# Twelve slots for the expert weights instead of eight, and a turn's buffers packed into 3592 columns

## What is computed

```python
xl = xl + g1l * (jnp.concatenate([a_lat, b_lat, c_lat], axis=-1) @ w_out[layer])
h2l = (rms_norm(xl, norm2_gain[layer]) * (1.0 + sc2l) + sh2l).reshape(-1, D_MODEL)
...
def hierarchical_moe(h, w_rg, b_rg, w_re, b_re, w_gate, w_up, w_down):
    g_logits = h @ w_rg + b_rg
    ...
    for gi in range(N_GROUPS):
        hid = jax.nn.silu(jnp.einsum('nd,edf->nef', h, w_gate[gi])) * jnp.einsum('nd,edf->nef', h, w_up[gi])
        y = y + jnp.einsum('nef,efd->nd', hid * comb[:, gi, :, None], w_down[gi])
    return y
```

## Time and profile before

| | |
|---|---|
| Median of 3 runs | 2015.53 us (2015.18 to 2016.91) |
| The profiled execution | 2014.9 us, its span 2013.1 us |
| Busy, share of the span | PE 85%, PEld 66%, DVE 43%, ACT 30%, POOL 6% |
| Moved by DMA | 419.94 MB, of it 417.87 MB on SP's queue |
| Mean granted TensorE clock | 0.936 |

### The profile page before, as it was taken

The page is one execution under the profiler, slowest core; times in us unless marked ns, Lnnn a source line. Parts: engine busy times, 40 slices in busy tenths (PEclk is TensorE's granted clock), DMA queues, the critical chain, the costliest instruction groups (busy, mean ns, idle before and its releaser), DMA issues.

```text
span 2013.1 us, 32404 instructions
## 1 busy us (share of the span) xinstructions
PE 1717.4 (85%) x14363; PEld 1325.0 (66%) x14363; DVE 868.9 (43%) x1199; ACT 596.6 (30%) x761; POOL 114.8 (6%) x103
## 2 busy tenths in 40 slices
PE   6999899999899989999999998696987666666665
PEld 6999898998699988899757554486854222122221
DVE  3445556663443556566414735867623111011111
ACT  4345445443334434554321020333313010000100
POOL 0500000000140000000032400000000000000000
PEclk9999999999899999999989998798998888888888
DMA  8651366745675236686333110000085999999998
GB/s 283 220 180 64 126 225 230 273 182 176 227 257 175 79 127 231 243 299 226 128 52 126 42 47 6 2 3 2 4 309 198 409 409 410 410 409 410 410 410 328
DMA packets 154814, 419.94 MB, mean 209 GB/s; under 512 B 13906, under 2 KB 20749, under 8 KB 151618
## 3 DMA queue, kind: packets, MB, share of 16 engines
q1 hardware_dynamic: 154402, 417.87, 56.1%
q10 hardware_dynamic: 288, 0.22, 0.0%
HBM read 416.18 MB, written 1.89 MB: 208 GB/s over the span
## 4 chain that ended last, share of the span: by engine, by line
PE 58%; DMA 17%; DVE 10%; SPq 7%; ACT 5%; issue 3%; DVEq 0%; ACTq 0%
PE bank L1174 28%; DMA wring<-w_exp_up 8%; SPq L1083 7%; DMA R<-w_exp_down 4%; PE ps_s L1284 3%; PE ps_t L1284 3%; PE bank L1362 3%; PE bank L1337 3%; PE ps_s L1337 3%; ACT w_high L1774 2%; DVE w_low L2178 2%; PE ps_t L1344 1%; DMA wring<-w_in 1%; PE bank L1729 1%; DMA wring<-w_up 1%
## 5 line engine op out<-in xcount | busy, mean ns | idle before, releaser
L2178 DVE TENSOR_TENSOR w_low<-wring,w_high 128x2048 fp32r<-128x2048 f32 (+1 forms) x128 | 287.2, 2244 | 330.9 <-ACT w_high L1774 330.2
L1774 ACT ACTIVATE w_high<-wring 128x2048 fp32r<-128x2048 f32 (+1 forms) x128 | 238.1, 1860 | 359.0 <-PE bank L1174 304.5
L1174 PE MATMUL bank<-x_high,w_high 128*128 128x256 f32 x1600 | 325.6, 285 | 18.3 <-DVEq L2206 11.5
L1174 PE MATMUL bank<-x_low,w_high 128*128 128x256 f32 x1600 | 321.6, 283 | 0.0
L1174 PE MATMUL bank<-x_high,w_low 128*128 128x256 f32 x1600 | 319.6, 281 | 0.0
L1174 PEld LDWEIGHTS bank<-x_high,w_high 128*128 128x128 f32 x1600 | 247.2, 191 | 25.9 <-DVEq L2206 12.5
L1174 PEld LDWEIGHTS bank<-x_high,w_low 128*128 128x128 f32 x1600 | 247.7, 190 | 0.0
L1174 PEld LDWEIGHTS bank<-x_low,w_high 128*128 128x128 f32 x1600 | 246.7, 190 | 0.0
L1729 PE MATMUL bank<-R 128*32 128x512 f32 x512 | 69.5, 674 | 38.8 <-DMA R<-w_exp_up 27.7
L1729 PE MATMUL bank<-wring,R 128*32 128x512 f32 x512 | 70.3, 685 | 34.6 <-DMA wring<-w_exp_up 34.6
L2827 DVE TENSOR_TENSOR R<-bank,R 128x512 f32<-128x512 f32 x8 | 5.5, 692 | 202.6 <-PE bank L1729 202.6
(11 more groups left out here) (581 smaller groups left out, 2759.6 us busy)
## 6 DMA issues: line engine op xcount, KB each, us to landing
wring<-w_in SPq DMA_DIRECT2D x37, 2048.0 KB, 8.0
wring<-w_up SPq DMA_DIRECT2D x22, 2048.0 KB, 8.2
R<-w_exp_gate SPq DMA_DIRECT2D x16, 2048.0 KB, 23.4
wring<-w_exp_gate SPq DMA_DIRECT2D x16, 2048.0 KB, 23.9
R<-w_exp_up SPq DMA_DIRECT2D x16, 2048.0 KB, 23.6
wring<-w_exp_up SPq DMA_DIRECT2D x16, 2048.0 KB, 24.1
R<-w_exp_down SPq DMA_DIRECT2D x16, 2048.0 KB, 23.6
wring<-w_exp_down SPq DMA_DIRECT2D x16, 2048.0 KB, 24.0
```

The costliest lines, as they stand in the source:

```text
L1174: mm = pe.matmul(b[:, i * S:(i + 1) * S], left, right, start=k == 0 and m == 0 and i == 0, stop=k == last and m == 2, skip_group_check=True)
L1774: a.activation(high_of(l, job), half_block(l, job, wring), ACT.Copy).then_inc(w_high_ready, 1)
L2178: v.tensor_tensor(half_block(l, job, w_low), half_block(l, job, wring), high_of(l, job).bitcast(F32), ALU.subtract).then_inc(w_low_ready, 1)
```

## The change

It raises `SLOTS_X` from 8 to 12. Slots 4 to 11 are now the last eight pieces of 4096 columns of R, which leaves 3592 columns for all that a turn needs. So the layout is rearranged:

- What a turn needs lies first in R: `gmoe` (the second half of the old `gmul`), `mod2`, `mulT`, then from `turn_area` on `xg`, `comb`, `posm`, `slot_no`, `pcol`, `ccol`, `pick`, `put`, `putT`, `hid`. `yg` shares its columns with `xg`; `sg` and `hidT` share theirs with `hid`. They overlay constants of the mixers (`base`) and `mixtok`.
- The router's buffers (`rl`, the selection, `moe_c`) start at `route_area` and lie in slot 11, `h2T` behind them in slots 11 and 10.
- The constants `c2_moe` come in two copies on ACT's queue, since `slot_no` now lies apart.
- DVE's markers are 3, 1, 2 as before, then 1 once `yb_ready` is reached, 2 and 1 in the output projection, 1 after the router's logits, and 1 after the first dispatch, behind a wait for `xs3_ready`: 12 in all. The first dispatch waits for the memset ahead of it, which now writes `pick`.
- `EXPERT_ORDER` names the slots in the order in which they come free.

```diff
-SLOTS, SLOTS_X = 4, 8
+SLOTS, SLOTS_X = 4, 12
...
-EXPERT_ORDER = (4, 2, 3, 5, 6, 7, 0, 1)
+EXPERT_ORDER = (4, 2, 3, 5, 6, 7, 8, 0, 9, 1, 10, 11)
...
         at[0] = 0
+        gmoe = part(D)
+        mod2 = part(2, KT)
+        mulT = part(3, KT)
+        turn_area = at[0]
         base = part(P + 64 + 18 * 64)
...
-        gmul = part(2, D)
+        gmix = part(D)
...
-        at[0] = x_area
-        h2T = part(KT, S)
+        at[0] = route_area
         rl = part(ST, 36)
...
+        ring_more = [R[:, R_SIZE - (i + 1) * BLOCK:R_SIZE - i * BLOCK] for i in range(more)]
+        assert at[0] <= R_SIZE - (more - 1) * BLOCK, (at[0], "router")
+        h2T = part(KT, S)
+        assert at[0] <= x_area
+
+
+        at[0] = turn_area
+        xg = part(KT, P)
+        yg = xg[:, :, :].rearrange("p k s -> p (k s)")
+        comb, posm = part(ST, N_EXP + QUAD), part(ST, N_EXP + QUAD)
...
-        xg = part(KT, P)
-        sg, hid = part(D_EXP), part(D_EXP)
-        hidT = part(D_EXP // P, P)
-        yg = part(D)
...
+        hid = part(D_EXP)
+        sg, hidT = hid, hid.rearrange("p (k s) -> p k s", k=D_EXP // P)
         assert at[0] <= R_SIZE - more * BLOCK, (at[0], "experts")
...
-            pe.wait_ge(moe_c_in, 16)
+            pe.wait_ge(moe_c_in, 32)
...
-            a.dma_start(moe_c, d["c2_moe"]).then_inc(moe_c_in, 16)
+            a.dma_start(moe_c, d["c2_moe"][:, 0:2 * P + S // SLOTS_E]).then_inc(moe_c_in, 16)
+            a.dma_start(slot_no, d["c2_moe"][:, 2 * P + S // SLOTS_E:]).then_inc(moe_c_in, 16)
...
             v.tensor_tensor(yv, yv, gg[:, :, :], ALU.mult).then_inc(yb_ready, 1)
+            v.wait_ge(yb_ready, 1)
+            v.memset(st[:, 61:62], 0.0).then_inc(moe_used, 1)
...
                 if j % 2 == 1:
-                    v.memset(st[:, 61:62], 0.0).then_inc(moe_used, 1)
+                    v.memset(st[:, 61:62], 0.0).then_inc(moe_used, 2 if j == 1 else 1)
...
             wait_emptied2(v, ("rt", 0))
+            v.memset(st[:, 61:62], 0.0).then_inc(moe_used, 1)
...
-            v.memset(st[:, 60:61], 0.0).then_inc(y_done, 4)
+            v.memset(pick[:, 0, 0:1], 0.0).then_inc(y_done, 4)
+            v.wait_ge(y_done, 4)
             dispatch(slice(0, QUAD))
+            v.wait_ge(xs3_ready, 2)
+            v.memset(order[:, 0:1], 0.0).then_inc(moe_used, 1)
```

More of the change, by code:

```diff
@@ L419, in second_constants @@
     moe[:, P:2 * P] = 1.0
-    moe[:, 2 * P:2 * P + SLOTS_E] = np.arange(SLOTS_E)
-    moe[:, 2 * P + SLOTS_E:] = SLOTS_E * np.arange(S // SLOTS_E)
+    moe[:, 2 * P:2 * P + S // SLOTS_E] = SLOTS_E * np.arange(S // SLOTS_E)
+    moe[:, 2 * P + S // SLOTS_E:] = np.arange(SLOTS_E)
     return {"c2_base": base, "c2_attn": attn, "c2_levels": hg, "c2_moe": moe}
@@ L647, in build @@
         rw_mask = base[:, P + 64:P + 64 + 18 * 64].rearrange("p (m t) -> p m t", t=64)
+        mixtok = part(ST, 768)
         cols2 = part(N_VEC2)
-        gmul = part(2, D)
+        gmix = part(D)
         lng = part(2, 64)
@@ L653, in build @@
         rbias = part(40)
-        mod2 = part(2, KT)
-        mulT = part(3, KT)
         gain2 = part(KT)
@@ L661, in build @@
         gup = part(B_W)
-        mixtok = part(ST, 768)
         st = part(80)
@@ L666, in build @@
         kam = part(2)
+        route_area = at[0]
         pB_r, pB_k, pB_v = part(2, S), part(2, T2), part(2, T2)
@@ L764, in build @@
         assert at[0] <= r_area
-        at[0] = x_area
-        h2T = part(KT, S)
+        at[0] = route_area
         rl = part(ST, 36)
-        comb = part(ST, N_EXP + QUAD)
         gsel, ge, gmx = part(ST, MG), part(ST, MG), part(ST)
@@ L772, in build @@
         sel1, sel2, m2, order = part(ST, PER_GROUP), part(ST, PER_GROUP), part(ST), part(PER_GROUP)
-        sel, posm = part(ST, N_EXP), part(ST, N_EXP + QUAD)
+        sel = part(ST, N_EXP)
         over = part(S // SLOTS_E)
         most, sweeps_f = part(1), part(1)
+        moe_c = part(2 * P + S // SLOTS_E)
+        earlier, all_ones, sweep_from = moe_c[:, 0:P], moe_c[:, P:2 * P], moe_c[:, 2 * P:]
+        more = SLOTS_X - SLOTS
+        ring_more = [R[:, R_SIZE - (i + 1) * BLOCK:R_SIZE - i * BLOCK] for i in range(more)]
[6 more added lines that the diff above has]
+        comb, posm = part(ST, N_EXP + QUAD), part(ST, N_EXP + QUAD)
         sweeps_i = part(1).bitcast(mybir.dt.int32)
-        moe_c = part(2 * P + SLOTS_E + S // SLOTS_E)
-        earlier, all_ones, slot_no = moe_c[:, 0:P], moe_c[:, P:2 * P], moe_c[:, 2 * P:2 * P + SLOTS_E]
-        sweep_from = moe_c[:, 2 * P + SLOTS_E:]
+        slot_no = part(SLOTS_E)
         pcol, ccol = part(ST, QUAD), part(ST, QUAD)
@@ L782, in build @@
         putT = part(ST, P)
-        xg = part(KT, P)
-        sg, hid = part(D_EXP), part(D_EXP)
-        hidT = part(D_EXP // P, P)
-        yg = part(D)
-        more = SLOTS_X - SLOTS
-        ring_more = [R[:, R_SIZE - (i + 1) * BLOCK:R_SIZE - i * BLOCK] for i in range(more)]
+        hid = part(D_EXP)
+        sg, hidT = hid, hid.rearrange("p (k s) -> p k s", k=D_EXP // P)
         assert at[0] <= R_SIZE - more * BLOCK, (at[0], "experts")
@@ L1903, in _ @@
                         for t in range(ST):
-                            a.activation(gmul[:, t, :], ctxb[:, t, :], ACT.Square, accum_out=st[:, 4 + t:5 + t]).then_inc(sumsq2, 1)
+                            a.activation((gmix, gmoe)[t], ctxb[:, t, :], ACT.Square, accum_out=st[:, 4 + t:5 + t]).then_inc(sumsq2, 1)
                     if l == DEPTH - 1 and j == 18:
@@ L2720, in _ @@
                 c = slice(half * 512, half * 512 + 512)
-                chain(v.tensor_tensor(tm, full_bank(("wout", j)), gmul[:, 0, c], ALU.mult))
+                chain(v.tensor_tensor(tm, full_bank(("wout", j)), gmix[:, c], ALU.mult))
                 v.tensor_tensor(h[:, t, c], h[:, t, c], tm, ALU.add).then_inc(dve_emptied2, 1)
```

4 lines of the change are left out of this document (2 added, 2 removed).

## The result

The changed kernel takes **1996.55 us** (median of 4 runs, 1991.78 to 1999.37) where the kernel before took 2015.55 on the same chip (4 runs, 2015.18 to 2016.91): a ratio of 0.990 with a 95% interval of 0.9887 to 0.9914, or 19.0 us less. The profiled execution took 1991.78 us, with a span of 1990.0, 23.1 us less than the span before. The forecast was 1995.2 us in a range of 1993.0 to 2000.5, so the median is within it (the profiled run alone, at 1991.78, is not).

The account below looks back on a forecast made before the run. The expert stage was taken as bound by its DMA bytes, 5.12 us per block. Four blocks (-20.5) and new steps (+0.2) took the profiled 2014.9 to 1994.6 us; 0.6 for the median gave 1995.2, range 1993.0 to 2000.5.

Parts of the forecast that it names:

- Four blocks, 20.5 us: Expert stage's load stream: 84 instead of 88 blocks remain from 1548 us on, 4 x 5.12 = 20.5 us less.
- load 12: One of the expert stage's 96 block loads, numbered 0 to 95; first to wait for an expert matmul, issued 1548.0 us.
- All four are moved in idle time: Before the first expert matmul: loads 6 to 11 fit between slot releases and 1548 us, with 4.4 us to spare.
- a last gap: Load queue just before the steady stream: empty for about 4.4 us before the load issued at 1548.0 us.
- The slack of load 11: Load into the last slot, issued at 1537.8 us: could go as late as 1543.6 without loss, 5.8 us of slack.
- The new steps, +0.2 us: DVE's added waits and markers: those behind router logits and at the first dispatch together cost 0.2 us, the others nothing.
- The constants, nothing: Two copies on ACT's queue instead of one: landed by about 1523.4 us, needed at 1532.84, so no cost.
- The sum, -20.3 us: Whole kernel: -20.5 us for the blocks and +0.2 us for DVE's new steps.
- B: Rival at SP's in-order loads: the last slot comes too late; losing a whole block gives 2000.3 us; chance 0.07.
- C: Rival at the expert loop's entry: code fetches wait behind the full DMA, 2018.9 us; chance 0.07.
- D: Rival at the slot markers: one is miscounted and nothing is loaded early, 2015.7 us; chance 0.01.
- the tail and the spread of runs: Term of the forecast's lower bound, for the kernel's end and scatter between runs: 1.0 us.

Follow-up runs that it names:

- dose runs: Changed kernel with 8, 10 or 12 blocks loaded before PE's first release: 467.5, 457.2 and 446.9 us from first expert matmul to the end.
- e8_hold11: Changed kernel with load 11 held until PE has done the first turn's gather and transposes: 1999.22 us, one run.
- e1_twelve: The changed kernel again without any edit, beside the other versions on their chip: 1995.63 us, ratio 0.990 to the kernel before.
- e10_twelve_b: The changed kernel again without any edit, in a later set on another chip: 1996.19 us, ratio 0.991 to the kernel before.
- e7_hold10: Changed kernel with loads 10 and 11 held until PE has used block 0: 2005.37 us, one run.
- e6_delay6: Changed kernel plus six DVE multiplications that nothing reads, ahead of the first dispatch: 1999.67 us, ratio 0.992 to the kernel before.
- e4_warm: Changed kernel plus unread PE matmuls, 15 before the token places and 6 before the first gather: 2000.37 us, ratio 0.992 to the kernel before.
- e9_warm7_b: Changed kernel plus 7 and 3 unread PE matmuls before token places and first gather, second set: 1994.71 us, ratio 0.990 to the kernel before.
- e5_warm7: Changed kernel plus 7 and 3 unread PE matmuls before token places and first gather, first set: 1994.11 us, ratio 0.989 to the kernel before.
- e3_packed8: Changed kernel's new layout with eight slots and the old slot order and markers: 2015.75 us, ratio 1.000 to the kernel before.

## Why the prediction was right

**Four blocks, 20.5 us: right.** From load 12's issue to the last landing the changed kernel takes 434.03 us where load 8 before took 454.32: 20.29 less for 84 blocks instead of 88. The dose runs put the block at 5.15 us.

**All four are moved in idle time: right**, as every issue that bears on it fell within 0.2 us of its place. I had a last gap of about 4.4 us and the windows show 4.7. The slack of load 11 was given as 5.8 us and is near 5.3, and here the prediction had a slip: 1552.2 - 8.6 = 1543.6 is the time at which load 12, not load 11, would have to be issued to follow without a gap. Load 11 delays load 12's landing (1556.6) only if it lands after 1556.6 - 5.12 = 1551.5, so if it is issued after 1542.9. From 1537.8 that is 5.1 us of slack, close to what e8_hold11 shows. No loss came of it, since load 11 went at 1534.8.

**The new steps, +0.2 us: right.** Load 12 is 2.80 us earlier than before where the loads ahead of it are 2.97 earlier: 0.17 us lost. From the start of L2803 to that of L2820, over the memset and the dispatch, DVE needs 1534.22 - 1532.85 = 1.37 us, against 1.27 before. The marker of the readout (1507.22) stands ahead of 4.32 us of waiting and costs nothing, as said; that behind the logits (1523.03) costs no more than 0.01.

**The constants, nothing: right, though they landed much later.** Both copies were beside the bulk loads on the way:

```profile
L2083 ACTq DMA_DIRECT2D R<-c_moe x1: 345/345/345, 1508.9 to 1508.9; - x1
...
DMA to landing us min/median/max: 6.3/6.3/6.3
L2084 ACTq DMA_DIRECT2D R<-c_moe x1: 450/450/450, 1509.3 to 1509.3; - x1
...
DMA to landing us min/median/max: 7.3/7.3/7.3
```

They landed after 6.3 and 7.3 us, with load 5 and load 6 on the way. The 3.4 us of before were not those of a quiet queue either, but the end of load 5 was all that was left there (it landed at 1514.9); 1509.3 + 7.3 = 1516.6, against a need at 1529.85. I had allowed for the whole of load 6 in front of them, 1523.4 on the axis of before.

**The sum, -20.3 us.** Between the two traces the part from load 3 to the end is 20.1 us shorter. The other 3.0 us of the 23.1 are not the change's: they arise before load 3, and the same changed kernel issues load 0 at 1466.6 in e1_twelve and at 1464.0 in e10_twelve_b, where it is 1461.0 in this trace and 1464.3 in that of before. The time at half clock before 1455 us doesn't explain them: it is 99.0 us in this trace and 105.8 in that of before, but e8_hold11, with only 95.6, issues load 0 at 1465.1, and e7_hold10, with 109.2, at 1464.7. Their cause stays open. The medians of three sets differ by 19.0, 20.0 and 18.0 us, and lie 0.4 to 1.4 us above the forecast's 1995.2. The Trainium skill's fit ("DMA: Bandwidth & Descriptors", "Anatomy of one DMA — SWDGE (gpsimd) path") would have made a block worth 6.8 us, and the whole 27.2. It is a fit for one DMA of the gpsimd path. These runs show that it can't be added up over SP's queued loads: they land 5.12 us apart in the trace and cost 5.15 us each in the dose runs.

**The rivals.** B (last slot late) didn't occur, but e8_hold11 shows its mechanism: load 11 issued 7.0 us later moved the last packet by 1.7. C (engines late into the loop) is false: PE's idle time ahead of the gather is 3.04 against 2.94 us, the first expert matmul 2.96 us earlier rather than later, and the turn after it starts after 2.50 us (2.49 before). So no stall at the loop's entry shows here, even with the DMA full. "Runtime: NRT & Kernel Launch" in the Trainium skill, "Instruction fetch mechanics", describes one for a taken branch whose target isn't in the fetched window; whether it lay outside here no row tells. D is false by the SP timeline.

**What was off is the spread.** I took 2015.18 to 2016.91 for the scatter of a run. In larger sets the kernel before runs from 2011.4 to 2021.1, and the changed one from 1991.8 to 1999.9. The range still held the median, but the profiled run fell 1.2 us below its lower bound, and 1.0 us for "the tail and the spread of runs" was too small. The upper bound of 2000.5 isn't the sum of its terms either: 1995.2 + 1.4 + 0.3 and a whole block of 5.1 give 2002.0. The highest run of the changed kernel was 1999.9. I had looked at the clock only as a mean.

## What to carry to other kernels

When a stage is bound by its bytes, as this one is, more buffers are worth just the blocks that they let in while the queue would otherwise stand, and nothing once it runs full; find the gap in the DMA share, find what ends it, and count the blocks that fit into it with their landing. After such a change the bottleneck ahead of the stage is another one: here the router's path, which had 18 us of empty queue behind it and now costs one us for each us that is added to it (taking 3.65 us off gave 3.1 back). To test this, change the dose (how many blocks go early) rather than only taking the change away.

## What was not expected of the hardware

**A tail that depends on the clock.** The last block's matmuls follow the last packet in 11.2 us in most traces, but in 12.6, 12.8, 12.9 and 14.1 us in four. In e6_delay6 PE's timeline begins to spread the last turn with:

```profile
1989.86 2.08 PE L1759 MATMUL ps_s<-R 128*128 128x512 f32 x2 [0.79 <-DVE R L2848]
1991.73 1.91 PE L1759 MATMUL ps_t<-R 128*128 128x512 f32 x2
```

The changed kernel's same rows, at 1982.02 and 1982.98, took 1.13 and 1.02 us. From 1455 us on every trace has stretches of half clock, 97 to 213 us in all, while PE waits for blocks again and again; whether one of them falls on the last block shifts the end by up to 3 us. In the four long tails one does: counted from the last packet it covers 0.9 to 4.3 us (e4_warm), 0.6 to 4.0 (e8_hold11), 0 to 4.9 (e9_warm7_b) and 1.5 to 8.3 (e6_delay6). In the other eight traces the first 9 us of the tail are at full clock. That is up to 3 us of the scatter between runs. Most of the rest arises before load 0, which is issued between 1461.0 and 1467.2 us in these traces; what makes it is open. I read this from the traces; no run sets the clock by itself, so it is an inference.

**Idle time ahead of a short step slows it.** The first gather takes 6.59 us in the changed kernel, where PE stood for 7.4 us from 1522.4 and the granted clock was at half from 1523.5 to 1540.6. It takes 3.73 and 3.84 us in e4_warm and e5_warm7, where PE was kept at work and the clock stayed full. A product of 128x128 by 128x512 in f32 takes 0.87 us at full clock.

**A small copy beside bulk loads lands later, but not behind all of them.** The two copies took 6.3 and 7.3 us. They landed at 1515.3 and 1516.6, after load 5 (1512.1) but ahead of load 6 (1517.6), which had been issued before them. In e3_packed8, where load 5 was the only block on the way, the same two copies took 2.1 and 3.2 us.
